# Moving the scaling of the normalised keys one doubling level earlier in VectorE's order

## The chip, the cores and the metric

The kernel runs on one core of a Trainium2 chip. The metric is the device time of one execution in microseconds (us), smaller is better. Two kernels are compared by the medians of runs that alternate on one chip.

## What is computed

The whole program is two networks, one after the other, each of depth 2, on 512 tokens of width 1024. The change lies in one part of the first network: the RWKV layer, a recurrence with a 64x64 state for each of 16 heads, run forward (d = 0) and backward (d = 1) over 256 context tokens and then 512 tokens. In short:

```python
kk = to_heads((k * k_k).astype(jnp.float32))
kk = kk * lax.rsqrt(jnp.sum(kk * kk, axis=-1, keepdims=True) + 1e-12)
...
def step(s, inp):                       # for each token, each head
    r_t, w_t, k_t, v_t, a_t, b_t = inp  # a_t = -kk, b_t = kk * a
    sa = jnp.einsum('bhvk,bhk->bhv', s, a_t)
    s = s * w_t[:, :, None, :] + sa[..., None] * b_t[:, :, None, :] + v_t[..., None] * k_t[:, :, None, :]
    return s, jnp.einsum('bhvk,bhk->bhv', s, r_t)
```

The normalised key `kk` is the quantity that matters here: both `a_t` and `b_t` of the recurrence are made of it. Mixture-of-experts layers stand before and after this part, and the second network (four kinds of attention and a feed-forward layer) follows.

## The kernel before

**Tiling.** The RWKV part works on pairs of heads, 128 channels at a time: `for p in range(KT)` with KT = 8, and in it `for d in range(2)`, the two directions. I call one (p, d) a half; there are 16. Tokens are cut into 12 chunks of 64 (NCH), handled in three groups b = 0, 1, 2 of four chunks (GC). While the chunks of direction d are being inverted and combined, the small vectors of the other direction, a = 1 - d, are prepared, so the two kinds of work alternate on every engine.

**The levels.** The triangular system of each chunk is inverted by doubling, in levels l = 1 to 5. For each level and each group, TensorE makes products (`level_products`, through the helper at line 1378) into a PSUM bank, VectorE masks the bank into the tile T (`level`, line 2768), TensorE makes two more products from T (`double_products`), and ScalarE copies them back (`level_copy`, line 2221). I write T(l,b) and XX(l,b) for them. The T banks are `"T": (2, 3, 2)`: T(l,2) uses the same PSUM bank as T(l,0). So TensorE may not start T(l,2) until VectorE has read T(l,0), and XX(l,0) needs T(l,0) too; the wait stands inside the loop over the middle levels:

```python
if b == 2:
    pe.wait_ge(lv_dve, i * 3 + ts)
```

**The order of the work.** Each engine runs its own list in order. `RK_DVE`, `RK_ACT`, `RK_PE` and `RK_POOL` write the order of the named steps out by hand; `rk_done(engine, p, step)` turns a step into a count of that engine's semaphore, which others wait for. The T and XX steps count on semaphores of their own.

**The keys.** At p, with d = 1, ScalarE squares the keys (line 2136), TensorE sums the squares by head, ScalarE takes logs (line 2156), and later, after its copies of level 1, does three things in this order: `key_factors` (line 2151, step `ka`), `key_roots` (line 2166, step `kr`: exp(-0.5 x) of the log, the reciprocal root) and `variance_roots` (line 2175, step `rs`). VectorE's `normed_keys` (line 2792, step `kkn`) waits for `kr` and multiplies the tile `kn` of 128x768 by the keys. Two consumers wait for `kkn`:

- GpSimd's `raw_keys`: it first waits for `ka` and multiplies `kd` by the keys (line 3246), then waits for `kkn` and multiplies `bd` by `kn` (line 3248). Behind it stand `keys_summed` (line 3254), `decayed_keys` (lines 3262 and 3263, which wait for ScalarE's step `exps`) and `decayed_queries` (line 3268).
- VectorE's own `decayed_sums` (line 2798), at level 3, which also waits for `exps`.

Both feed TensorE's `scores`, which come after level 5.

**Around it on VectorE.** At level 1 of a half stand the T steps, three steps of the sequential chain between chunks (`chain`, line 2776, named z) and `scan` (line 2783). With d = 1, level 2 is T(2,0), T(2,1), T(2,2), `normed_keys`, `normed` (line 2823, step `yn`, which belongs to the output of the previous pair), and then level 3 begins.

Of the kernel before, what the change touches and what calls it, by code (L numbers as in the profile page):

```python
# [100 lines left out]
for _d in range(2):  # L101
    _a = 1 - _d
    _z = [("z", _a, _j) for _j in range(1, 12)]
    _zs = lambda n: [_z.pop(0) for _ in range(min(n, len(_z)))]
    RK_PE += [("vt", 0), ("vt", 1)] if _d == 0 else []
    RK_PE += [("x0", _d, 0), ("pre", _a, 0), ("pre", _a, 1), ("x0", _d, 1), ("x0", _d, 2)] + _zs(1)
    RK_PE += [("mv", _d, 0)] + _zs(1) + [("mv", _d, 1)] + _zs(1) + [("mv", _d, 2)] + _zs(1)
    RK_PE += [("kn", 0)] * _d + _zs(_d) + [("kn", 1), ("var",)] * _d
    for _l in range(1, 6):
        _n = _l in (1, 5)  # L110
        RK_PE += [("T", _d, _l, 0), ("T", _d, _l, 1)] + _zs(_n) + [("T", _d, _l, 2), ("XX", _d, _l, 0)] + _zs(_n)
        RK_PE += [("XX", _d, _l, 1)] + _zs(_l == 5) + [("XX", _d, _l, 2)] + _zs(_n)
    RK_PE += [("gate",), ("bonus",)] * _d
    assert not _z
    RK_PE += [("sb", _a, 0), ("sk", _a, 0), ("wu", _d, 0), ("ba", _a, 0), ("kt", _a, 0), ("sb", _a, 1), ("sk", _a, 1)]
    RK_PE += [("wu", _d, 1), ("wu", _d, 2)] + ([] if _d else [("mean",)]) + [("ba", _a, 1), ("kt", _a, 1)]
    RK_PE += [("ar", _d, 0), ("kv", _d, 0), ("sb", _a, 2), ("sk", _a, 2), ("bc", _d, 0), ("ar", _d, 1), ("kv", _d, 1)]
    RK_PE += [("ba", _a, 2), ("kt", _a, 2), ("bc", _d, 1), ("y", _d, 1), ("kv", _d, 2), ("ar", _d, 2), ("bc", _d, 2), ("y", _d, 2)]

    RK_DVE += [("pp",)] if _d else []  # L120
    _z = [("z", _a, _j) for _j in range(1, 11)] + [("yf", _a)]
    RK_DVE += [("et", _d)] + [("x0", _d, _b) for _b in range(3)] + _zs(EARLY[_d])
    for _l in range(1, 6):
        _more = {1: [[("scan", _a)], []], 2: [[("kkn",), ("yn",)] * _d, []], 3: [[("ara", _a)], []], 4: [[], [("res1",), ("lnx",)] if _d else [("ksr",)]], 5: [[], []]}[_l]
        RK_DVE += _zs(_l in (1, 5)) + _zs(_l in (1, 5)) + _more[0] + _zs(_l in (1, 5)) + _more[1] + _zs(_l == 5)
    assert not _z
    RK_DVE += [("res",), ("bonus",)] * _d + [("mt", _a, 0)]
    RK_DVE += [("mt", _a, 1)] + ([] if _d else [("cen",)]) + [("ar", _d, 0), ("mt", _a, 2), ("bc", _d, 0)]
    RK_DVE += [("ar", _d, 1), ("bc", _d, 1), ("y", _d, 1), ("ar", _d, 2), ("bc", _d, 2), ("y", _d, 2), ("zi", _d)]

    RK_ACT += [] if _d else [("vt", 0), ("vt", 1)]
    RK_ACT += [("pw", _a), ("pa", _a), ("pwc", _a), ("pac", _a)] + [("kq",)] * _d
    RK_ACT += [("mv", _d, _b) for _b in range(3)] + [("kn", 0), ("kn", 1), ("var",)] * _d
    RK_ACT += [("ka", _a)] + [("kr",), ("rs",)] * _d + [("exps", _a)] + [("aff",)] * _d
    RK_ACT += [("nt", _a, 0), ("wu", _d, 0), ("ba", _a, 0), ("kt", _a, 0), ("nt", _a, 1), ("wu", _d, 1), ("wu", _d, 2)]
    RK_ACT += [("ba", _a, 1), ("kt", _a, 1)] + ([] if _d else [("sq",)]) + [("nt", _a, 2), ("ba", _a, 2), ("kt", _a, 2)]

    RK_POOL += [("kdk", _a), ("bdk", _a), ("ksm", _a), ("bds", _a), ("kds", _a), ("arr", _a), ("qm", _a, 1), ("qm", _a, 2)]
    LV_DVE += [("T", _d, _l, _b) for _l in range(1, 6) for _b in range(3)]
    LV_ACT += [("XX", _d, _l, _b) for _l in range(1, 6) for _b in range(3)]  # L140
    LV_POOL += [("nl", _d, _b) for _b in range(3)] + [("ni", _d, _b) for _b in range(3)]
# [76 lines left out]
for _u in range(len(ATTENTION)):  # L218
    _more = _u + 1 < len(ATTENTION)
# [180 lines left out]
def build(nc, slabs_d, vecs_d, tabs1_d, tabs2_d, aux_d, lora_d, x_d, ctx_d, out_d, kv_d):  # L400
# [5 lines left out]
    with stack:  # L406
# [48 lines left out]
        def cut(whole, at, *shape):  # L455

            n = math.prod(shape)
            v = whole[:, at:at + n]
            if len(shape) == 2:
                v = v.rearrange("p (a b) -> p a b", a=shape[0])  # L460
            if len(shape) == 3:
                v = v.rearrange("p (a b c) -> p a b c", a=shape[0], b=shape[1])
            return v
# [117 lines left out]
        lnx, o = cut(work, o, 2), o + 2  # L581
# [21 lines left out]
        ksr, o = cut(work, o, NX), o + NX  # L603
# [173 lines left out]
        def rk_done(engine, p, *name):  # L777

            order = {"pe": RK_PE, "dve": RK_DVE, "act": RK_ACT, "pool": RK_POOL}[engine]
            return {"pe": rk_pe, "dve": rk_dve, "act": rk_act, "pool": rk_pool}[engine], rk_count(order, p, name)  # L780
# [1649 lines left out]
        def _(v):  # L2430
# [100 lines left out]
            for f in range(KT):  # L2531
                for part in range(2):
# [10 lines left out]
                    d = v.drain()  # L2543
# [194 lines left out]
            def column(n):  # L2738
                return pp[:, n:n + 1]
# [5 lines left out]
            def parameters(p):  # L2745

                v.tensor_copy(lnxn, pp[:, 7:9])
                v.drain()
                v.tensor_copy(pp[:, 0:9], rwp[:, bass.ds(p + 1, 1), :].rearrange("p a b -> p (a b)"))
                v.drain()  # L2750
                v.tensor_scalar(column(9), column(5), -1.0, 1.0, ALU.mult, ALU.add).then_inc(rk_dve, rk.next("pp"))

            def totals(p, d):

                v.wait_ge(*rk_done("act", p - 1 if d == 0 else p, "exps", d))
                v.tensor_copy(ETd[d], ETa[d]).then_inc(rk_dve, rk.one("et", d))

            def first_levels(p, d):

                for b in range(3):  # L2760
                    v.wait_ge(*rk_done("pe", p, "x0", d, b))
                    v.tensor_tensor(X[:, GC * b:GC * b + GC, :], rk_bank("x0", d, b)[:, 0:256].rearrange(CHUNKED, c=GC),
                                    bc(eye2.unsqueeze(1), 128, GC, CH), ALU.add).then_inc(rk_dve, rk.one("x0", d, b))
# [25 lines left out]
            def normed_keys(p):  # L2789

                v.wait_ge(*rk_done("act", p, "kr"))
                v.scalar_tensor_tensor(kn, ktile, column(4), kn, ALU.mult, ALU.mult).then_inc(rk_dve, rk.next("kkn"))
# [92 lines left out]
            for p in range(KT):  # L2885
                for d in range(2):
                    a = 1 - d
                    if d == 1:
                        parameters(p)
                    totals(p, d)  # L2890
                    first_levels(p, d)
                    for j in range(1, EARLY[d] + 1):
                        chain(p, a, j)
                    steps = iter(range(EARLY[d] + 1, NCH))
                    for l in range(1, 6):
                        level(p, d, l, 0)
                        level(p, d, l, 1)
                        if l in (1, 5):
                            chain(p, a, next(steps))
                        level(p, d, l, 2)  # L2900
                        if l in (1, 5):
                            chain(p, a, next(steps))
                        if l == 1:
                            scan(p, a)
                        elif l == 2 and d == 1:
                            normed_keys(p)
                            normed(p)
                        elif l == 3:
                            decayed_sums(p, a)
                        if l in (1, 5):  # L2910
                            chain(p, a, next(steps))
                        if l == 5 and d == 0:
                            chain(p, a, next(steps))
                        if l == 4:
                            if d == 1:
                                with_bonus(p)
                                v.tensor_copy(lnx, lnxn).then_inc(rk_dve, rk.one("lnx"))
                            else:
                                weighted_keys(p)
                    if d == 1:  # L2920
                        gated(p)
                        bonuses(p)
                    masked_scores(p, a, 0)
                    masked_scores(p, a, 1)
                    if d == 0:
                        centred(p)
                    transitions(p, d, 0)
                    masked_scores(p, a, 2)
                    additions(p, d, 0)
                    for b in (1, 2):  # L2930
                        transitions(p, d, b)
                        additions(p, d, b)
                    first_state(p, d)
                assert rk.rest() == 0
# [605 lines left out]
```

## Time and profile before

| | |
|---|---|
| median of 3 runs | 4296.15 us |
| lowest, highest run | 4291.41, 4308.15 us |
| the profiled execution's own time | 4308.15 us |
| its span, first to last instruction | 4306.3 us |
| TensorE busy, share of the span | 3907.4 us, 91% |
| VectorE, ScalarE, GpSimd busy | 38%, 20%, 17% |
| the RWKV halves | from about 1240 to 2028 us of the span |

Busy time is the time in which an engine executes something; an engine that is idle because another is late is not busy. What an engine waited for is given as the releaser: the engine and line whose end let it go on. "Issue" is TensorE waiting for nothing that the profile names. The profile prints rows with line numbers of the kernel; TensorE's products all carry the line of a helper (1378 for pairs of heads, 907 for plain products), so their place is read from the time and from the engines around them.

### The profile page before, as it was taken

The page shows a single profiled execution, that of the slowest core. Times are in us where ns is not written, and L with a number is a line of the kernel's source. Part 1 is how long each engine was busy: PE and PEld are TensorE (multiplying, and loading weights), DVE is VectorE, ACT ScalarE, POOL GpSimd, SP SyncE. Part 2 cuts the span into 40 slices and gives each one's busy share as a digit, 9 for nine tenths or more (in the row PEclk, how much of TensorE's full clock was granted, in tenths as well). Part 3 has the DMA queues.
Part 4 walks back from the last instruction along what each step waited for, and adds up shares of the span by engine and source line. Part 5 has one row for each costly group of instructions (what it writes and reads, how often), then busy time and mean ns, then how long its engine had stood idle before and what let it go on. Part 6 is the DMA issues. An engine that isn't in the chain of part 4 may idle for free.

```text
span 4306.3 us, 93568 instructions
## 1 busy us (share of the span) xinstructions
PE 3907.4 (91%) x39960; PEld 2506.7 (58%) x39960; DVE 1636.1 (38%) x3343; ACT 850.4 (20%) x1847; POOL 750.8 (17%) x601
## 2 busy tenths in 40 slices
PE   5979999989978888888899998999999989999998
PEld 4534444445557777777344443456688854658887
DVE  2412112144445554444222222453444425516353
ACT  2200000020045555444100001214000011420000
POOL 4100000000033433333000000000334300004343
PEclk8989999999989999999899999999999999999999
DMA  8287887862200000000379995110222211002221
GB/s 336 98 305 298 334 332 298 334 253 92 81 7 12 12 17 12 12 12 12 137 330 429 429 429 244 40 59 1 79 79 81 94 69 47 32 20 84 93 79 39
DMA packets 54202, 619.10 MB, mean 144 GB/s; under 512 B 5648, under 2 KB 8976, under 8 KB 18320
## 3 DMA queue, kind: packets, MB, share of 16 engines
q1 hardware_dynamic: 49664, 599.41, 35.3%
q10 hardware_dynamic: 2448, 9.05, 0.6%
q0 software_dynamic: 1792, 6.29, 0.5%
q8 instruction: 234, 3.83, 0.4%
q14 instruction: 64, 0.52, 0.0%
HBM read 602.40 MB, written 12.32 MB: 143 GB/s over the span
## 4 chain that ended last, share of the span: by engine, by line
PE 44%; issue 43%; DVE 4%; DMA 3%; POOLq 3%; POOL 2%; ACT 1%; DVEq 1%; PEld 0%; SPq 0%; ACTq 0%; PEldq 0%
PE bank L907 30%; PE bank L1378 13%; DMA ring<-slabs 2%; POOL work L3316 1%; POOLq L3319 1%; POOLq L3317 1%; DMA kv<-work 1%; POOLq L3206 1%; POOL work L3320 1%; PE bank L1429 1%; DVE work L2768 1%; DVE work L2448 0%; DVE hc L2508 0%; DVE hc L2509 0%; PEld bank L907 0%
## 5 line engine op out<-in xcount | busy, mean ns | idle before, releaser
L907 PE MATMUL bank<-ring,work 128*32 128x256 f32 (+3 forms) x7002 | 764.0, 438 | 69.4 <-DMA ring<-slabs 57.3
L907 PE MATMUL bank<-work 128*128 128x256 f32 (+8 forms) x3590 | 782.0, 428 | 26.4 <-DVE work L3132 16.7
L907 PEld LDWEIGHTS bank<-work 128*128 128x128 f32 (+3 forms) x3590 | 499.0, 184 | 298.4 <-issue 213.5
L907 PEld LDWEIGHTS bank<-ring,work 128*32 128x32 f32 (+2 forms) x7002 | 316.5, 123 | 491.8 <-issue 394.6
L907 PE MATMUL bank<-work,ring 128*128 128x256 f32 (+1 forms) x1616 | 482.6, 457 | 13.4 <-DVE work L3151 5.1
L907 PE MATMUL bank<-hx,ring 128*128 128x512 f32 (+1 forms) x1344 | 482.8, 515 | 6.6 <-DVE hx L2463 4.5
L907 PEld LDWEIGHTS bank<-work,ring 128*128 128x128 f32 x1616 | 307.1, 191 | 183.9 <-issue 135.0
L907 PEld LDWEIGHTS bank<-hx,ring 128*128 128x128 f32 x1344 | 255.9, 192 | 221.3 <-issue 200.4
L1378 PE MATMUL bank<-work 64*64 64x64 f32 x11520 | 322.8, 225 | 63.4 <-issue 48.5
L1378 PEld LDWEIGHTS bank<-work 64*64 64x64 f32 x11520 | 288.8, 138 | 91.1 <-issue 88.7
L3209 POOL TENSOR_TENSOR work<-work 128x512 f32<-128x512 f32 (+1 forms) x30 | 34.4, 1155 | 1470.2 <-ACT work L1980 1470.2
L2439 DVE TENSOR_TENSOR work<-work,bank 128x256 f32<-128x256 f32 x240 | 91.8, 416 | 396.0 <-ACT work L2417 391.7
L2417 ACT ACTIVATE work<-bank 128x256 f32<-128x256 f32 x48 | 18.4, 383 | 725.3 <-PE bank L907 725.3
L2221 ACT ACTIVATE work<-bank 128x512 f32<-128x512 f32 (+1 forms) x240 | 127.8, 553 | 166.2 <-PE bank L1378 163.3
L3315 POOL TENSOR_TENSOR work<-ring 128x512 f32<-128x512 f32 (+1 forms) x48 | 78.7, 1640 | 459.8 <-PE bank L907 429.9
L2768 DVE TENSOR_TENSOR work<-bank,tabs_sb 128x256 f32<-128x256 f32 x240 | 100.9, 424 | 121.0 <-PE bank L1378 118.0
L1378 PE MATMUL bank<-ring,work 64*64 64x64 f32 (+1 forms) x3168 | 113.7, 250 | 34.2 <-issue 19.0
L2656 DVE TENSOR_TENSOR work<-work,bank 128x256 f32<-128x256 f32 x16 | 6.8, 422 | 323.9 <-PE bank L907 323.9
L3132 DVE SCALAR_TENSOR_TENSOR work<-work 128x256 f32<-128x256 f32 x176 | 123.6, 717 | 16.3 <-issue 6.8
L907 PE MATMUL bank<-resc,work 128*128 128x256 f32 x512 | 121.3, 380 | 4.3 <-POOL work L3315 3.9
L1378 PEld LDWEIGHTS bank<-ring,work 64*64 64x64 f32 x3168 | 97.1, 137 | 47.9 <-issue 46.8
L907 PE MATMUL bank<-hx,work 128*128 128x256 f32 x512 | 121.1, 379 | 0.4 <-POOL work L3316 0.4
(320 smaller groups left out, 4781.6 us busy)
## 6 DMA issues: line engine op xcount, KB each, us to landing
ring<-slabs SPq DMA_DIRECT2D x228, 2048.0 KB, 9.7
work<-slabs SPq DMA_DIRECT2D x48, 2048.0 KB, 18.3
work<-kv SPq DMA_DIRECT2D x18, 384.0 KB, 3.1
kv<-work SPq DMA_DIRECT2D x2, 3072.0 KB, 15.7
kv<-work ACTq DMA_DIRECT2D x6, 512.0 KB, 17.7
work<-tabs ACTq DMA_DIRECT2D x1, 2176.0 KB, 8.7
resx<-xT SPq DMA_DIRECT2D x1, 2048.0 KB, 11.1
outT<-hx ACTq DMA_DIRECT2D x8, 256.0 KB, 2.1
```

The source lines that it names most:

```text
L907: return pe.matmul(out, lhsT, rhs, start=(k == 0), stop=(k == n - 1))
L1378: m = pe.matmul(out[other if across else r], lhsT[r], rhs[r], start=first, stop=last)
L1429: pe.matmul(outw[:, 0:n], wa2[two[d], 0:128], HW[two[d], at:at + n], start=True, stop=True)
L2221: act.activation(dst, bank, ACT.Copy).then_inc(lv_act, 1)
L2439: v.tensor_tensor(out, a, b, op)
L2768: v.tensor_tensor(T[d][:, GC * b:GC * b + GC, :], rk_bank("T", d, l, b)[:, 0:256].rearrange(CHUNKED, c=GC), bc(levels[:, 1 - d, l, :].unsq ...
L3132: return v.scalar_tensor_tensor(dst, x, 1.0, y, ALU.mult, ALU.subtract)
L3206: pool.drain()
L3315: pool.tensor_tensor(s3, a["a11"], a["a21"], ALU.subtract).then_inc(ff_pool, 1)
L3316: pool.tensor_tensor(s1, a["a21"], a["a22"], ALU.add).then_inc(ff_pool, 1)
L3317: pool.drain()
L3319: pool.drain()
```

## The change

The call of `normed_keys(p)` moves, on VectorE, from behind T(2,2) of level 2 to the end of level 1, behind the third chain step, ahead of T(2,0). The hand-written order `RK_DVE` moves its step `kkn` in the same way, so that all counts of the semaphore agree. The instruction itself, its operands and its wait for `kr` are the same, and no other engine's list is touched. It concerns the halves with d = 1: eight calls.

```diff
@@ RK_DVE, the order of VectorE's steps
-        _more = {1: [[("scan", _a)], []], 2: [[("kkn",), ("yn",)] * _d, []], 3: [[("ara", _a)], []], ...
+        _more = {1: [[("scan", _a)], [("kkn",)] * _d], 2: [[("yn",)] * _d, []], 3: [[("ara", _a)], []], ...
@@ VectorE, in the loop over the levels
                         if l == 1:
                             scan(p, a)
                         elif l == 2 and d == 1:
-                            normed_keys(p)
                             normed(p)
                         elif l == 3:
                             decayed_sums(p, a)
@@
                             chain(p, a, next(steps))
                         if l == 5 and d == 0:
                             chain(p, a, next(steps))
-                        if l == 4:
+                        if l == 1 and d == 1:
+                            normed_keys(p)
+                        elif l == 4:
                             if d == 1:
                                 with_bonus(p)
```

## Rows read from the trace of the kernel before

**Rows 1.** Busy time and granted clock by stretch: all RWKV halves.
```profile
core 0: us, PE busy (x) PEld busy (x) DVE busy (x) ACT busy (x) POOL busy (x), PEclk, DMA share, GB/s
1240.00:2028.00 788.00, 655.37 (x21942) 570.01 (x21942) 381.85 (x844) 401.76 (x751) 301.52 (x309) 0.98 0.05 13
```

**Rows 2.** Timeline of VectorE, second half of p = 1: start, duration, line.
```profile
1394.62 0.28 DVE L2776 SCALAR_TENSOR_TENSOR work<-bank,work,hc 128x64 f32<-128x64 f32 x1 [1.17 <-PE bank L1378]
1395.14 0.89 DVE L2768 TENSOR_TENSOR work<-bank,tabs_sb 128x256 f32<-128x256 f32 x2 [0.23 <-PE bank L1378]
1396.43 0.42 DVE L2768 TENSOR_TENSOR work<-bank,tabs_sb 128x256 f32<-128x256 f32 x1 [0.40 <-PE bank L1378]
1396.77 1.90 DVE L2792 SCALAR_TENSOR_TENSOR work<-work 128x768 f32<-128x768 f32 x1
1398.59 0.68 DVE L2823 TENSOR_TENSOR work<-work 128x512 f32<-128x512 f32 x1
1399.64 0.89 DVE L2768 TENSOR_TENSOR work<-bank,tabs_sb 128x256 f32<-128x256 f32 x2 [0.37 <-PE bank L1378]
```

**Rows 3.** Timeline of ScalarE, same stretch.
```profile
1394.92 1.03 ACT L2151 ACTIVATE work<-work 128x768 f32<-128x768 f32 x1
1395.84 0.84 ACT L2166 ACTIVATE work<-work 128x768 f32<-128x768 f32 x1
```

**Rows 4.** Timeline of GpSimd, same half.
```profile
1396.03 1.82 POOL L3246 TENSOR_TENSOR work<-work 128x768 f32<-128x768 f32 x1 [13.58 <-ACT work L2151]
1398.75 2.21 POOL L3248 TENSOR_TENSOR work<-work 128x768 f32<-128x768 f32 x1 [0.90 <-DVE work L2792]
...
1405.96 1.73 POOL L3268 TENSOR_TENSOR ring<-work 128x512 f32<-128x512 f32 x1
```

**Rows 5.** Timeline of TensorE, same half: level 2, and the first scores.
```profile
1394.42 2.29 PE L1378 MATMUL bank<-work 64*64 64x64 f32 x67
1396.92 0.96 PE L1378 MATMUL bank<-work 64*64 64x64 f32 x45 [0.21 <-issue]
...
1412.66 1.56 PE L1378 MATMUL bank<-ring,work 64*64 64x64 f32 x48
```

**Rows 6.** Timelines of VectorE and ScalarE: p = 0, 4 and 7, level 2.
```profile
1297.39 0.89 DVE L2768 TENSOR_TENSOR work<-bank,tabs_sb 128x256 f32<-128x256 f32 x2
1298.16 0.83 ACT L2166 ACTIVATE work<-work 128x768 f32<-128x768 f32 x1
...
1693.08 0.41 DVE L2768 TENSOR_TENSOR work<-bank,tabs_sb 128x256 f32<-128x256 f32 x1
1695.64 0.42 DVE L2768 TENSOR_TENSOR work<-bank,tabs_sb 128x256 f32<-128x256 f32 x1 [0.36 <-PE bank L1378]
...
2003.99 0.89 DVE L2768 TENSOR_TENSOR work<-bank,tabs_sb 128x256 f32<-128x256 f32 x2 [0.39 <-PE bank L1378]
2005.62 1.01 DVE L2792 SCALAR_TENSOR_TENSOR work<-work 128x768 f32<-128x768 f32 x1
2003.50 0.83 ACT L2166 ACTIVATE work<-work 128x768 f32<-128x768 f32 x1
```

**Rows 7.** TensorE at p = 0, level 2, and the instruction queue beside it.
```profile
1300.11 1.64 PE L1378 MATMUL bank<-work 64*64 64x64 f32 x65 [1.00 <-issue]
...
q8 instruction: 1, 0.02, 1.9%
```

**Rows 8.** Stretches of p = 5 with TensorE's granted clock, and T(3,0), T(4,0) there.
```profile
1798.00:1801.30 3.30, 1.88 (x51) 1.67 (x53) 1.16 (x3) 2.04 (x5) 2.52 (x2) 1.00 0.00 0
1801.30:1804.70 3.40, 3.40 (x116) 3.33 (x113) 1.30 (x2) 2.13 (x4) 2.67 (x2) 0.50 0.00 0
...
1800.26 0.89 DVE L2768 TENSOR_TENSOR work<-bank,tabs_sb 128x256 f32<-128x256 f32 x2 [1.96 <-PE bank L1378]
1805.07 0.89 DVE L2768 TENSOR_TENSOR work<-bank,tabs_sb 128x256 f32<-128x256 f32 x2 [2.13 <-PE bank L1378]
```

**Rows 9.** Timeline of VectorE, p = 1: T(4,0) and T(4,1).
```profile
1403.65 0.89 DVE L2768 TENSOR_TENSOR work<-bank,tabs_sb 128x256 f32<-128x256 f32 x2 [1.10 <-PE bank L1378]
```

**Rows 10.** Who waited for whom in the RWKV halves: total, times, longest.
```profile
PE bank L1378 <- issue: 105.6, 128, 2.4
```

More of the change, by code:

```diff
@@ L123 @@
     for _l in range(1, 6):
-        _more = {1: [[("scan", _a)], []], 2: [[("kkn",), ("yn",)] * _d, []], 3: [[("ara", _a)], []], 4: [[], [("res1",), ("lnx",)] if _d else [("ksr",)]], 5: [[], []]}[_l]
+        _more = {1: [[("scan", _a)], [("kkn",)] * _d], 2: [[("yn",)] * _d, []], 3: [[("ara", _a)], []], 4: [[], [("res1",), ("lnx",)] if _d else [("ksr",)]], 5: [[], []]}[_l]
         RK_DVE += _zs(_l in (1, 5)) + _zs(_l in (1, 5)) + _more[0] + _zs(_l in (1, 5)) + _more[1] + _zs(_l == 5)
```

## The prediction, made before the changed kernel was run

> **What bounds the kernel now.** I read the busy shares of the RWKV stretch first, then the timelines of the engines over one half with d = 1, then who waited for whom. In the stretch of 788 us TensorE is busy for 655 us, VectorE and ScalarE for about half, GpSimd for 38% [rows 1]. TensorE is the engine whose list sets the end, and most of what it loses it loses to "issue" [rows 10]. But busy VectorE time is not free: TensorE may only go on inside a level when VectorE has emptied T. So the question is where in VectorE's list the instruction of line 2792 is late for somebody, not how long it takes.
>
> At p = 1 VectorE ends chain step z8 at 1394.90, starts T(2,0) at 1395.14, T(2,1) follows, T(2,2) starts at 1396.43, `kkn` (line 2792) at 1396.77 and takes 1.90 us, `yn` ends at 1399.27, and T(3,0) starts at 1399.64, after an idle 0.37 us that TensorE ended [rows 2]. So where `kkn` stands today, it and `yn` fill a hole in which VectorE would wait for TensorE: it costs the path nothing. Its input `kr` on ScalarE ends at 1396.68 [rows 3], 0.09 us before `kkn` starts. The new place is the one before T(2,0), at 1394.90: 1.78 us before its input exists.
>
> **The change part by part.**
>
> *The consumers of kkn.* GpSimd's line 3246 waits for `ka` alone and ends at 1397.85; line 3248 starts 0.08 us after `kkn` [rows 4]. What earlier start can they get? None at p = 1: `kkn` already starts 0.09 us after its input. At p = 4 and p = 7, `kkn` starts behind T(2,2), 1.3 us and more after `kr` (2005.62 against 2004.33) [rows 6], so there it could be up to 1.3 us earlier. But line 3268, the last thing that `scores` needs from GpSimd, ends at 1407.69, and the scores start at 1412.66, when level 5 is through [rows 4, 5]. There are 5 us of slack, so an earlier `kkn` is worth 0. The other consumer, at level 3, waits for `exps` as well, which comes behind level 2. I credit nothing.
>
> *The hole that it leaves.* 0, since T(3,0) was waiting for TensorE [rows 2].
>
> *The new place, p = 1.* VectorE comes to `kkn` at 1394.90 and waits until 1396.68 + 0.09 = 1396.77. So it starts when it started before. Behind it on VectorE now stand T(2,0), T(2,1) and T(2,2), and for T(2,0) TensorE waits twice (the shared bank of T(2,2), and XX(2,0)).
>
> How long does `kkn` take there? Durations are 1.90 us at p = 1 and 1.01 us at p = 7 [rows 2, 6]. At p = 1 GpSimd's line 3246 runs beside it until 1397.85 and `kkn` ends at 1398.67, 0.82 us later [rows 2, 4]. At p = 7 it started 1.3 us after `kr`, when line 3246 was nearly through. Since the new place ties the start to `kr` and line 3246 to `ka`, one ScalarE instruction ahead of it, every pair gets the relation of p = 1. I take 1.90 us for all eight; the bound below is 1.01.
>
> The Trainium skill (SBUF — State Buffer, Who interferes with whom) says that a VectorE instruction with two SBUF inputs and a GpSimd instruction that reads SBUF exclude each other for the whole instruction. By that rule `kkn` cannot end before the GpSimd instruction has ended plus its own work, which is what the 0.82 us at p = 1 look like; without the rule it would be 1.01 us for all.
>
> So T(2,0) starts, by the overlap of 0.08 us that is usual between two VectorE rows, at `kr`'s end + 0.09 + 1.90 - 0.08, that is `kr` + 1.91. From T(2,0) to T(2,2) it is 1.29 us (1395.14 to 1396.43), which is the eviction, the release and TensorE's eight pairs of products [rows 2]. T(2,2) therefore starts at `kr` + 3.20. At p = 1: 1396.68 + 3.20 = 1399.88, against 1396.43: 3.45 us late.
>
> The same for all pairs, from the end of `kr` and the start of T(2,2): p = 0 (1298.99, 1298.68) 3.51; p = 1 3.45; p = 2 3.35; p = 3 2.86; p = 4 (1694.55, 1695.64) 2.11; p = 5 2.84; p = 6 1.65; p = 7 (2004.33, 2005.28) 2.25 [rows 2, 3, 6]. At p = 4 TensorE's own stall had already pushed T(2,2) 2.56 us behind T(2,0) [rows 6], so part of the wait is hidden there. Sum 22.0 us. Everything behind T(2,2) hangs on it in a chain (XX, copy, next T), and `exps`, GpSimd and the scores move along by the same amount, so I see no slack in the half that gives it back. One stall of 0.4 us in level 2 of p = 1, after a fetch of instructions that is by then over, drops out: the row at 1396.92 [rows 5]. That leaves **21.6 us**.
>
> *The clock.* TensorE now stands still for about 3.4 us in level 2. In the trace of before, such breaks bring its clock down: at p = 5 TensorE was busy for 1.88 of 3.30 us, and in the next 3.40 us the granted clock was 0.50, 1.2 GHz in place of 2.4 GHz [rows 8]. What one such stretch costs: T(3,0) to T(4,0) took 4.81 us there and 4.01 us at full clock at p = 1 [rows 2, 8, 9]: 0.80 us. The bounds are none more, and two more per half (16 x 0.80 = 12.8 us). I take six: at p = 6 and p = 7 there is a stretch at half clock already, and elsewhere the break will mostly be long enough. 6 x 0.80 = **4.8 us**.
>
> Sum: 21.6 + 4.8 = **+26.4 us**. The profiled execution took 4308.15 us and would take 4334.6. It is itself 12 us above the median of 4296.15, so I set the sum on the median: **4322.5 us**, a ratio of 1.006.
>
> **The rivals.** 0.5% is 21.5 us, and about the least that a measurement of this kernel can tell from no change; I use it as the border.
>
> *A. TensorE's fetches of instructions hide part of the wait.* For this speaks that TensorE in this stretch idles for "issue" 128 times, 105.6 us in all [rows 10]. An example is the 1.00 us before 1300.11, level 2 of p = 0, with one packet of the instruction queue just before it [rows 7]. Stalls of this kind, of 1.0 to 1.5 us, stand behind T(2,2) at p = 0, 5, 6 and 7, about 5 us together. If the fetch went on while TensorE waits, these would be gone: 22.0 - 0.4 - 5 = +16.6 us, and with fewer breaks at half clock about +19, so 4315. Against it: the fetch of p = 0 starts after TensorE has passed the wait for T(2,0), so it is tied to the place in the code, and the place doesn't move.
>
> The Trainium skill (Runtime: NRT & Kernel Launch, Instruction fetch mechanics) says that the sequencer fetches the next block while it executes the present one and that this is mostly hidden. The trace disagrees on "hidden", with its 105.6 us of issue.
>
> *B. kkn takes 1.01 us in its new place.* Then each delay is 0.89 us less: 22.0 - 7.1 = +14.9 us, and with shorter breaks and two or three stretches at half clock +17, so 4313. For this speak the rows of 1.01 us, against it the relation to line 3246 above.
>
> *C. The change does next to nothing.* This would be if the 5 us of slack before the scores belonged not to GpSimd alone but to TensorE, that is if something else than the chain of levels set the start of the scores. I see nothing in the rows that does. It would give 0 to +5 us, 4299.
>
> *D. Faster.* One mechanism: GpSimd's lines 3248, 3262, 3263 and 3268 set the start of the scores in the later pairs, where `kkn` gets up to 1.3 us earlier. It would decide if line 3268 ended at the start of the scores and not 5 us ahead, and if `kr` were there before z8 ends. Price: at most 3 pairs x 1 us, -3 us, 4293, and only with the loss at T(2,0) away. The row of `kr` speaks against it at every pair.
>
> **How the numbers follow.** Chances: the forecast (wait in full, some half clock; its own range +20 to +34 us, 4316 to 4330) 0.65; A 0.15; B 0.09; C 0.08; D 0.03. For the range, the lower end must take in B and A with some of the spread between executions (the three runs lie 17 us apart), the upper end two more half-clock stretches per half (21.6 + 12.8 = +34.4): 4307 to 4331, which leaves out C, D and a little of the ends. Slower by over 0.5% needs more than +21.5 us: most of the forecast's share (0.85 of it), and a third of A's and a tenth of B's: about 0.62. The rest of these and C are within 0.5%: 0.35. Faster: 0.03.
>
> **What the new profile would show.** In the halves with d = 1: `kkn` directly behind z8 with 1 to 2 us of idle VectorE time before it, released by ScalarE's line 2166, in eight places; its duration near 1.90 us in all eight; T(2,0) directly behind it, with no idle time; from the end of `kr` to the start of T(2,2) 3.20 us; TensorE idle 3 us or more ahead of T(2,2), named as released by VectorE or as issue; and more stretches at clock 0.50 right behind. GpSimd's line 3248 starts no earlier relative to `kr`. The halves with d = 0 and everything outside 1240 to 2028 us keep their length. I am wrong if `kr` comes earlier on ScalarE than today (nothing in ScalarE's list changes), if `kkn` takes 1.0 us there, if the issue stalls behind T(2,2) vanish, or if the halves grow by less than T(2,2) is late.

## The result, and the profile after

| kernel | median, us | range, us | runs |
|---|---|---|---|
| before | 4296.41 | 4289.33 to 4308.15 | 8 |
| after | 4317.77 | 4302.49 to 4331.86 | 8 |

The ratio is 1.0051, with a 95% interval of 1.0035 to 1.0068: the changed kernel is 21.4 us slower. The first experiment, with other runs of both kernels, gives 1.0048, 1.0027 to 1.0068. The forecast was 4322.5 us. The profiled execution of after took 4321.99 us; its span is 4320.2 us. In the changed kernel GpSimd's lines 3246, 3248 and 3268 have the numbers 3247, 3249 and 3269; VectorE's and ScalarE's lines named here keep theirs.

VectorE's timeline of after, second half of p = 1, answers to [rows 2]. Columns: start, duration, line, in brackets the idle time before and who ended it.

```profile
1396.73 0.28 DVE L2776 SCALAR_TENSOR_TENSOR work<-bank,work,hc 128x64 f32<-128x64 f32 x1 [2.08 <-PE bank L1378]
1398.61 1.93 DVE L2792 SCALAR_TENSOR_TENSOR work<-work 128x768 f32<-128x768 f32 x1 [1.60 <-ACT work L2166]
1400.46 0.74 DVE L2768 TENSOR_TENSOR work<-bank,tabs_sb 128x256 f32<-128x256 f32 x2
1401.74 0.42 DVE L2768 TENSOR_TENSOR work<-bank,tabs_sb 128x256 f32<-128x256 f32 x1 [0.54 <-PE bank L1378]
1402.08 0.91 DVE L2823 TENSOR_TENSOR work<-work 128x512 f32<-128x512 f32 x1
1404.99 0.42 DVE L2768 TENSOR_TENSOR work<-bank,tabs_sb 128x256 f32<-128x256 f32 x1 [2.01 <-PE bank L1378]
```

The third chain step ends, VectorE stands idle for 1.60 us until ScalarE's line 2166 (`kr`) is there, `kkn` takes 1.93 us, and T(2,0) follows with no idle time. Before, `kkn` and `yn` filled VectorE's wait for TensorE; now VectorE waits there 2.01 us and the time is empty.

GpSimd's timeline of the same half, for [rows 4]:

```profile
1397.92 1.80 POOL L3247 TENSOR_TENSOR work<-work 128x768 f32<-128x768 f32 x1 [14.96 <-ACT work L2151]
1400.62 1.82 POOL L3249 TENSOR_TENSOR work<-work 128x768 f32<-128x768 f32 x1 [0.90 <-DVE work L2792]
```

ScalarE's, for [rows 3]:

```profile
1397.75 0.83 ACT L2166 ACTIVATE work<-work 128x768 f32<-128x768 f32 x1
```

`kkn` starts 0.03 us after `kr` ends (1398.58) and ends 0.82 us after GpSimd's line 3247 does (1399.72), as at p = 1 before. GpSimd's line 3249 starts 2.04 us behind the end of `kr`, against 2.07 before (1398.75 against 1396.68) [rows 3, 4]: the consumer gets nothing.

All instructions of line 2792 in after (count, then minimum, median and maximum duration in ns), and the idle time before them:

```profile
L2792 DVE SCALAR_TENSOR_TENSOR work<-work x9: 1932/1935/1941, 1214.4 to 2022.5; 128x768 f32<-128x768 f32 x9
its engine sat idle before it (us, times) until:
  ACT work L2166: 16.1, 9
```

Nine, since one belongs to the prologue: 1.93 us in every one.

TensorE, after. The first row is from p = 1, the second from p = 0; the idle time in brackets is the break in level 2.

```profile
1401.02 6.16 PE L1378 MATMUL bank<-work 64*64 64x64 f32 x224 [2.98 <-DVE work L2768]
...
1299.80 5.41 PE L1378 MATMUL bank<-work 64*64 64x64 f32 x155 [3.63 <-DVE work L2768]
```

Busy time by stretch, after, p = 0: the break, and what follows it. Columns as in [rows 1]; the tenth is TensorE's granted clock.

```profile
1296.20:1299.60 3.40, 0.00 (x0) 0.00 (x0) 2.22 (x3) 1.67 (x3) 2.02 (x2) 1.00 0.02 5
1299.60:1303.00 3.40, 3.20 (x97) 3.16 (x101) 1.74 (x4) 0.91 (x2) 2.17 (x2) 0.50 0.02 5
```

The same at p = 1, where the break ends at 1401.02:

```profile
1398.60:1402.00 3.40, 0.98 (x51) 1.01 (x55) 2.85 (x4) 0.49 (x1) 2.50 (x2) 1.00 0.00 0
1402.00:1405.40 3.40, 3.40 (x104) 3.33 (x97) 1.39 (x3) 2.42 (x4) 1.46 (x2) 0.50 0.03 7
```

At p = 0 TensorE stands still for the whole of the first stretch and runs the second at half clock (0.50, 1.2 GHz). From T(2,0) to T(2,2) it is 1.71 us there (1299.24 to 1300.95). At p = 1 that piece is still at full clock and takes 1.28 us (1400.46 to 1401.74), as it did before [rows 2]; half clock follows 0.98 us after the break.

From p = 4 on the idle time is in two pieces, since a stall for instructions stands just ahead of the break. TensorE at p = 5:

```profile
1815.61 0.62 PE L1378 MATMUL bank<-work 64*64 64x64 f32 x13 [1.07 <-issue]
1818.55 2.72 PE L1378 MATMUL bank<-work 64*64 64x64 f32 x78 [2.33 <-DVE work L2768]
```

**Where the time went.** The RWKV stretch, measured in each trace from the first instruction of VectorE's line 2762 to the last T(5,0), before:

```profile
1236.70:2018.04 781.34, 650.43 (x21808) 566.07 (x21810) 379.08 (x839) 400.90 (x749) 304.54 (x314) 0.98 0.04 13
```

after:

```profile
1235.02:2038.17 803.15, 659.54 (x21818) 576.14 (x21822) 386.07 (x840) 401.94 (x749) 302.98 (x314) 0.96 0.04 12
```

Who TensorE waited for there, in us, times, longest; before:

```profile
PE bank L1378 <- issue: 105.0, 127, 2.4
PE bank L1378 <- DVE work L2768: 6.6, 14, 1.6
```

after:

```profile
PE bank L1378 <- issue: 100.7, 117, 2.8
PE bank L1378 <- DVE work L2768: 25.1, 15, 3.6
```

Each kernel was profiled a second time (the first and the fifth experiment). The means of the two profiles:

| in the RWKV stretch, us | before | after | difference |
|---|---|---|---|
| length | 782.0 | 804.1 | +22.1 |
| TensorE waits for line 2768 (T) | 6.2 | 25.9 | +19.7 |
| TensorE waits for issue | 105.2 | 99.2 | -6.0 |
| TensorE busy, same products | 652.1 | 661.9 | +9.8 |
| of it at half clock (counted in the trace's record of the clock) | 39.3 | 76.8 | +37.5 |

The three differences make +23.5 of the +22.1 us. The halves with d = 1 together went from 384.4 and 380.5 us to 405.0 and 405.6, those with d = 0 from 396.9 and 402.1 to 398.2 and 399.5. Outside the stretch nothing changed in one direction. The two first profiles differ by only 13.9 us in span because there after was 1.7 us shorter ahead of the stretch and 6.2 us behind it; the stretch holds what the medians show.

### The profile page after: what moved, and what is told of

Same layout as the page of the kernel before. It is cut to its first block, busy times and chain, and to the rows that moved or that the text cites. A ratio compares the mean times of both kernels' runs of the same rounds, so it can differ in the third digit from the quotient of the medians.

```text
span 4320.2 us, 93568 instructions
## 1 busy us (share of the span) xinstructions
PE 3907.6 (90%) x39960; PEld 2505.7 (58%) x39960; DVE 1642.4 (38%) x3343; ACT 851.3 (20%) x1847; POOL 749.6 (17%) x601
## 4 chain that ended last, share of the span: by engine, by line
PE 44%; issue 43%; DVE 4%; DMA 3%; POOLq 3%; POOL 2%; ACT 1%; DVEq 1%; PEld 0%; SPq 0%; ACTq 0%; PEldq 0%
PE bank L907 30%; PE bank L1378 13%; DMA ring<-slabs 2%; POOL work L3317 1%; POOLq L3320 1%; POOLq L3318 1%; DMA kv<-work 1%; POOLq L3207 1%; POOL work L3321 1%; PE bank L1429 1%; DVE work L2768 0%; DVE work L2792 0%; DVE work L2448 0%; DVE hc L2508 0%; DVE hc L2509 0%
## 5 line engine op out<-in xcount | busy, mean ns | idle before, releaser
L1378 PE MATMUL bank<-work 64*64 64x64 f32 x11520 | 332.6, 232 | 80.3 <-issue 47.1
L1378 PEld LDWEIGHTS bank<-work 64*64 64x64 f32 x11520 | 300.6, 143 | 107.4 <-issue 104.8
L3210 POOL TENSOR_TENSOR work<-work 128x512 f32<-128x512 f32 (+1 forms) x30 | 34.4, 1156 | 1465.8 <-ACT work L1980 1465.8
L1378 PE MATMUL bank<-ring,work 64*64 64x64 f32 (+1 forms) x3168 | 111.3, 248 | 31.5 <-issue 17.0
L3133 DVE SCALAR_TENSOR_TENSOR work<-work 128x256 f32<-128x256 f32 x176 | 123.6, 717 | 16.3 <-issue 6.8
```

The source lines that it names most:

```text
L1378: m = pe.matmul(out[other if across else r], lhsT[r], rhs[r], start=first, stop=last)
L3133: return v.scalar_tensor_tensor(dst, x, 1.0, y, ALU.mult, ALU.subtract)
```

## The experiments

The ratio is always to the kernel before, timed in turn with it on the same chip; its median there was 4299.32 us beside experiments 1 to 4, 4296.60 beside 5 to 8, and 4301.99 beside 9 and 10. The ratio is not exactly that of the two medians. The stretch is the one above; means of two profiles for before and after, one profile for the others.

| experiment | median, us | ratio, 95% interval | stretch | waits for T | half clock |
|---|---|---|---|---|---|
| before | 4296.41 | | 782.0 | 6.2 | 39.3 |
| after | 4317.77 | 1.0051, 1.0035 to 1.0068 | 804.1 | 25.9 | 76.8 |
| 1 after again | 4318.23 | 1.0048, 1.0027 to 1.0068 | (in after) | | |
| 2 wait only | 4308.90 | 1.0012, 0.9995 to 1.0029 | 787.8 | 11.8 | 47.8 |
| 3 kr early | 4303.03 | 1.0003, 0.9989 to 1.0018 | 782.5 | 9.1 | 34.1 |
| 4 GpSimd late | 4318.54 | 1.0037, 1.0018 to 1.0055 | 792.3 | 22.1 | 44.4 |
| 5 before again | 4298.66 | 0.9995, 0.9976 to 1.0013 | (in before) | | |
| 6 after, unrolled | 4333.72 | 1.0088, 1.0060 to 1.0115 | 816.4 | 31.5 | 88.7 |
| 7 6 with filler | 4317.08 | 1.0050, 1.0032 to 1.0069 | 803.8 | 16.3 | 37.5 |
| 8 before, unrolled | 4298.18 | 1.0004, 0.9986 to 1.0021 | 776.5 | 4.5 | 41 |
| 9 behind the scan | 4306.77 | 1.0008, 0.9994 to 1.0023 | 777.3 | 7.5 | 37.5 |
| 10 copy late | 4298.41 | 0.9998, 0.9977 to 1.0020 | 777.8 | 2.1 | 27.3 |

### 1 and 5. Both kernels again

No edit. They show how far two profiles of one kernel lie apart in the sums above.

> The changed kernel itself once more, for a second profile of it. Theory (the wait): T(2,0) stands on VectorE behind an instruction whose input comes late; T(2,2) starts 3.6 us after kr ends in all eight halves with d = 1, kkn takes 1.93 us, and the halves with d = 1 are together 20 us longer than before, while the rest of the program differs only by what two executions of one kernel differ. Rival (the loss is spread, by the clock): the 20 us would be found in other places than in the first profile. Time expected: 4318 us, ratio 1.005.

> The kernel before itself, for a second profile of it. It says how far two executions of one kernel differ in the RWKV halves: from the first row of line 2762 to the last T(5,0) it was 781.3 us in the first profile, against 803.2 and 806.4 us in the two profiles of the changed kernel. Theory (the difference is the change's): within 4 us of 781. Rival (half of it is chance): near 790. Ratio 1.000.

After: +18.9 us, stretch 805.1 us (the second expectation, written later, gives 806.4). From the end of `kr` to T(2,2) it is 3.60, 3.17, 3.60, 3.61, 3.61, 3.54, 3.17 and 3.61 us, so the 3.6 us expected in all eight halves come in six, and in the first profile in seven (p = 1 has 3.16). The 20 us are again in the halves with d = 1. Before against itself: 0.9995. The same kernel has a stretch of 781.3 or 782.6 us, 803.2 or 805.1 us. Two profiles each show the spread only in part: experiments 8, 9 and 10, whose times are those of before, have stretches of 776.5 to 777.8 us. A difference of under 5 us in one profile is therefore not read as a gain or a loss.

### 2. The wait without the work

```diff
 # the kernel before, VectorE, level 1, behind the third chain step
+                        if l == 1 and d == 1:
+                            v.wait_ge(*rk_done("act", p, "kr"))
```

> Half of the move: VectorE waits for kr at the new place, ahead of T(2,0), but kkn itself is executed at its old place behind T(2,2). Theory (wait and work both count): T(2,0) starts 0.1 us after kr's end and T(2,2) 1.4 us after it; from the trace of before that is late by 1.7, 1.6, 1.5, 1.0, 0.3, 1.0, 0 and 0.4 us, 7.6 us in all, and kkn takes 1.0 us since line 3246 on GpSimd is through: 4304 us, ratio 1.0018. Rival (the wait for kr is all of it, and kkn's work hides behind TensorE): ratio 1.005 as in the full change. Rival (it is all kkn's work): no change.

VectorE, p = 0:

```profile
1298.12 0.76 DVE L2768 TENSOR_TENSOR work<-bank,tabs_sb 128x256 f32<-128x256 f32 x2 [1.79 <-ACT work L2166]
1299.41 0.42 DVE L2768 TENSOR_TENSOR work<-bank,tabs_sb 128x256 f32<-128x256 f32 x1 [0.53 <-PE bank L1378]
1299.76 1.01 DVE L2792 SCALAR_TENSOR_TENSOR work<-work 128x768 f32<-128x768 f32 x1
```

VectorE waits as long as in after, T(2,0) starts when `kr` ends, and T(2,2) comes 1.32 us behind it (1.76 at p = 2). The stretch grows by 5.8 us, against 7.6 expected. The ratio makes it some 5 us, with an interval that does not tell it from none; the medians lie 9.6 us apart. `kkn` behind T(2,2) takes 1.01 us in every half, since GpSimd's instruction is by then mostly through. The wait alone is thus about a quarter of the loss, as far as one profile tells.

### 3. The work without the wait

```diff
 # the changed kernel, ScalarE: kr right behind the variance logs, ahead of the level-1 copies and of ka
-    RK_ACT += [("mv", _d, _b) for _b in range(3)] + [("kn", 0), ("kn", 1), ("var",)] * _d
-    RK_ACT += [("ka", _a)] + [("kr",), ("rs",)] * _d + [("exps", _a)] + [("aff",)] * _d
+    RK_ACT += [("mv", _d, _b) for _b in range(3)] + [("kn", 0), ("kn", 1), ("var",), ("kr",)] * _d
+    RK_ACT += [("ka", _a)] + [("rs",)] * _d + [("exps", _a)] + [("aff",)] * _d
                         variance_logs(p)
+                        key_roots(p)
...
                         if l == 1 and d == 1:
-                            key_roots(p)
                             variance_roots(p)
```

> The changed kernel with its input made early: key_roots stands on ScalarE directly behind the logs, ahead of the copies of level 1, where ScalarE waits for TensorE. Theory (wait and work both count): VectorE no longer waits at kkn; kkn starts right behind z8 and takes 1.0 us because it is done before line 3246 on GpSimd starts. T(2,0) is late by about 0.8 us a half and some of it is hidden behind stalls of TensorE: +5 us, 4301 us, ratio 1.0012. Rival (kkn's work is the cost, 1.9 us wherever it stands ahead of T(2,0)): +12 us, 1.003. Rival (something else in the new order than T(2,0) costs, such as GpSimd's earlier line 3248): still 1.005.

VectorE, p = 1:

```profile
1393.78 0.28 DVE L2776 SCALAR_TENSOR_TENSOR work<-bank,work,hc 128x64 f32<-128x64 f32 x1 [1.16 <-PE bank L1378]
1393.97 1.01 DVE L2792 SCALAR_TENSOR_TENSOR work<-work 128x768 f32<-128x768 f32 x1
1394.90 0.75 DVE L2768 TENSOR_TENSOR work<-bank,tabs_sb 128x256 f32<-128x256 f32 x2
```

With its input there, `kkn` starts as soon as the chain step is done, takes 1.01 us, and T(2,0) starts 0.84 us behind the chain step in place of 0.24. The stretch is 782.5 us and the time that of before (5 us more were expected, which the interval still allows). The place in VectorE's list alone is not what costs; it is the place together with an input that is late and a neighbour that blocks.

### 4. GpSimd's instruction behind kkn

```diff
 # the changed kernel, GpSimd
                 pool.wait_ge(*rk_done("act", p, "ka", d))
-                pool.tensor_tensor(kd, kd, ktile, ALU.mult).then_inc(rk_pool, rk.next("kdk", d))
                 pool.wait_ge(*rk_done("dve", p if d == 0 else p - 1, "kkn"))
+                pool.tensor_tensor(kd, kd, ktile, ALU.mult).then_inc(rk_pool, rk.next("kdk", d))
```

> The changed kernel with GpSimd's line 3246 behind the wait for kkn, so that it can't run beside kkn. Theory (kkn's 1.93 us are 1.01 us of work and 0.92 us of waiting for GpSimd's instruction): kkn takes 1.01 us in all eight halves, T(2,2) starts 2.7 us after kr's end in place of 3.6, 7.4 us less than the changed kernel in all and somewhat less half clock; GpSimd starts 2 us later and has 5 us of slack: about +13 us, 4309 us, ratio 1.003. Rival (GpSimd's chain has no slack): ratio 1.005 or more, with TensorE's scores waiting for line 3268.

All instructions of line 2792:

```profile
L2792 DVE SCALAR_TENSOR_TENSOR work<-work x9: 1018/1019/1020, 1213.6 to 2012.7; 128x768 f32<-128x768 f32 x9
```

VectorE at p = 0:

```profile
1295.81 1.02 DVE L2792 SCALAR_TENSOR_TENSOR work<-work 128x768 f32<-128x768 f32 x1 [1.79 <-ACT work L2166]
```

TensorE, p = 0:

```profile
1297.30 1.61 PE L1378 MATMUL bank<-work 64*64 64x64 f32 x80 [2.71 <-DVE work L2768]
```

Busy time by stretch, the break and what follows it:

```profile
1294.50:1297.30 2.80, 0.10 (x4) 0.03 (x1) 1.50 (x3) 1.79 (x3) 0.33 (x1) 1.00 0.03 6
1297.30:1300.70 3.40, 3.05 (x137) 2.84 (x139) 1.53 (x4) 1.82 (x4) 3.40 (x2) 1.00 0.02 5
```

TensorE at p = 5, and its clock there:

```profile
1801.63 0.62 PE L1378 MATMUL bank<-work 64*64 64x64 f32 x13 [0.80 <-issue]
1803.93 2.26 PE L1378 MATMUL bank<-work 64*64 64x64 f32 x80 [1.68 <-DVE work L2768]
...
1801.20:1804.60 3.40, 1.29 (x44) 1.18 (x48) 1.69 (x3) 1.72 (x3) 1.01 (x1) 1.00 0.00 0
1804.60:1808.00 3.40, 2.96 (x97) 2.55 (x86) 1.31 (x2) 1.19 (x2) 3.40 (x3) 0.51 0.02 5
```

`kkn` still waits for `kr`, but takes 1.02 us in place of 1.93: the 0.9 us in each half belong to GpSimd's instruction beside it. The stretch is 792.3 us, 11.8 us less than in after, of which the waits for T give only 3.8 us in the sums, and 8.7 us are TensorE's busy time (653.2 against 661.9 us): behind a break of 2.71 us the granted clock at p = 0 stayed 1.00, and behind after's 3.63 us it was 0.50. It stayed full in the halves p = 0 to 3; in p = 4, 5 and 6, where a stall for instructions of 0.72 to 1.72 us stands ahead, half clock comes 0.6 to 1.0 us behind the end of breaks of only 0.79 to 1.81 us, and in p = 7 between a stall of 1.36 us and the break. The expectation of +13 us for the stretch was 2.7 us high. GpSimd's later work did not become late: its last instruction for the scores ended at 1308.79, the scores began at 1313.76. The times do not show this gain: the ratio of 1.0037 makes it some 16 us over before, against 10.3 in the stretch, the interval overlaps that of after, and the median is 4318.54 us where after, beside it, had 4318.23. That the loss is about halved rests on the stretch of one profile.

### 6. Level 2 written out: the fetches moved

```diff
 # the changed kernel, TensorE, middle levels
+                first = 2 + (d == 1)
+                if d == 1:
+                    level_t(p, d, 2, 0)
+                    level_t(p, d, 2, 1)
+                    level_t(p, d, 2, 2)
+                    for b in range(3):
+                        level_x(p, d, 2, b)
...
-                with pe.Fori(0, 3) as i:
+                with pe.Fori(0, 5 - first) as i:
```

> The changed kernel with TensorE's level 2 of the halves with d = 1 written out ahead of the loop (the loop then runs over levels 3 and 4 alone). The waits are the same; the code is longer by one level per half with d = 1, and the places where TensorE fetches instructions move. It is the control for the next run. Theory: T(2,2) still starts 3.6 us after kr's end, half clock in the RWKV halves stays near 70 to 85 us, ratio 1.005 plus up to 0.002 for eight or so more fetches of about 1 us.

The same products run in the same order, but TensorE's code lies elsewhere, and so do the places at which it runs dry. The changed kernel is now slower than expected: ratio 1.0088 against at most 1.007, stretch 816.4 us, half clock 88.7 us against 70 to 85. What of this is the move of `kkn`, experiment 8 shows.

### 7. The same, with filler products in the break

```diff
 # experiment 6, TensorE
                     level_t(p, d, 2, 1)
+                    pe.wait_ge(*rk_done("dve", p, "z", 0, 8))
+                    for _ in range(4):
+                        mm(P[6][:, 256:512], headones, tab("level")[:, 0:256], 0, 1)
                     level_t(p, d, 2, 2)
```

The four products write a part of a bank that nobody reads; their result goes nowhere. They wait for the third chain step.

> As the run before it, with four products of 128x128 by 256 columns, whose result nobody reads, put between TensorE's T(2,1) and its wait for T(2,0): about 2 us of work inside a wait of 3.8 us. The wait is as long as before; only TensorE's idleness is gone. Theory (a third to a half of the loss is TensorE at 1.2 GHz after the idle stretch): T(2,2) starts 3.2 us after kr in place of 3.6, half clock in the RWKV halves falls to 35 to 45 us, and the kernel is 6 to 9 us faster than the unrolled one. Rival (the clock costs nothing, the wait is all): the same time as the unrolled one.

TensorE, p = 0 (line 2778 is T's line 2768 in this kernel):

```profile
1284.07 1.99 PE L907 MATMUL bank<-tabs_sb 128*128 128x256 f32 x8
1287.91 1.29 PE L1378 MATMUL bank<-work 64*64 64x64 f32 x59 [1.85 <-DVE work L2778]
```

The break is 1.99 us of filler (eight records for the four products) and 1.85 us of idle time in place of one break. VectorE's list, and so its lateness, is that of experiment 6, and the time falls by 16.6 us in the medians and by 12.6 us in the stretch; the time at half clock falls from 88.7 to 37.5 us, that of before. From the end of `kr` to T(2,2) it is 3.17 us in seven halves of eight, where after had 3.60. The expectation was 6 to 9 us. The filler also moves the code behind it, and experiment 8 shows how much a layout can do; but the time for issue went up by 3.0 us (101.1 to 104.1), so that isn't where the gain came from. TensorE's busy time, with about 16 us of filler in it, fell from 665.8 to 663.3 us. So I put 12 us and more of the cost in experiment 6 down to the clock, 0.25 us of stretch for each us at half clock (12.6 by 51.2).

### 8. The kernel before with level 2 written out

The edit of experiment 6 on the kernel before.

> The kernel before with the same unrolling of level 2. With the unrolled changed kernel it gives the cost of the move a second time, in code whose fetches stand elsewhere. Theory: the difference between the two is 18 to 25 us, as between the originals; the unrolling alone costs 0 to 8 us. Rival (the cost of the move depends on where the fetches fall): a difference well under 15 us or over 28 us.

1.0004: writing level 2 out costs nothing by itself. The move of `kkn`, put on top, costs 35.5 us in the medians and 39.9 us in the stretch (776.5 to 816.4), where it costs 21.4 and 22.1 in the first layout. In the parts: waits for T +27.0 us (4.5 to 31.5), busy +17.5 us (648.3 to 665.8), issue -3.3 us (104.4 to 101.1). The rival of this expectation was right. By the busy time a us at half clock is dearer here, 0.37 us (17.5 by 47.7). What such a move costs depends on the layout of TensorE's code, and with it on where TensorE runs dry of instructions by itself.

### 9. kkn behind the scan, with kr early

The kernel before, with experiment 3's edit on ScalarE, and on VectorE:

```diff
                             scan(p, a)
+                            if d == 1:
+                                normed_keys(p)
                         elif l == 2 and d == 1:
-                            normed_keys(p)
                             normed(p)
```

> An earlier place than the change's, with the input early as in the third run: key_roots directly behind the logs on ScalarE, and kkn on VectorE directly behind scan, ahead of chain step z8, where VectorE waits for TensorE in most halves. Theory (a place costs what of wait and work lies beyond the hole it fills): kkn takes 1.01 us, fills VectorE's wait for z8, T(2,0) isn't late, TensorE's waits for line 2768 are about 7 us in the RWKV halves as before, and the ratio is 1.000. Rival (anything of 1 us ahead of T(2,0) costs, input early or not): ratio 1.001 to 1.002.

VectorE, p = 1:

```profile
1392.05 1.77 DVE L2783 TENSOR_TENSOR_SCAN work<-tabs_sb,work 128x780 f32<-128x780 f32 x1
1393.74 0.99 DVE L2792 SCALAR_TENSOR_TENSOR work<-work 128x768 f32<-128x768 f32 x1
1394.99 0.28 DVE L2776 SCALAR_TENSOR_TENSOR work<-bank,work,hc 128x64 f32<-128x64 f32 x1 [0.26 <-PE bank L1378]
1395.51 0.89 DVE L2768 TENSOR_TENSOR work<-bank,tabs_sb 128x256 f32<-128x256 f32 x2 [0.23 <-PE bank L1378]
```

Here `kkn` fills VectorE's wait ahead of the third chain step (0.26 us of it is left) and costs nothing that can be measured: 1.0008, with an interval of 0.9994 to 1.0023 that does not shut out the rival by itself; the stretch of 777.3 us, no longer than before's, speaks against it. I take it as no better than the old place either, since no consumer waits for `kkn`.

### 10. The copy of line 2917 later

The kernel before, with the step `lnx` at the end of level 5 in place of level 4. In the trace of before this copy of 128x2 elements takes 1.24 us in level 4; VectorE's timeline, p = 1:

```profile
1406.48 1.24 DVE L2917 COPY work<-work 128x2 f32<-128x2 f32 x1
```

It ends at 1407.72, and GpSimd's line 3268 ends at 1407.69 [rows 4].

```diff
                                 with_bonus(p)
-                                v.tensor_copy(lnx, lnxn).then_inc(rk_dve, rk.one("lnx"))
...
+                        elif l == 5 and d == 1:
+                            v.tensor_copy(lnx, lnxn).then_inc(rk_dve, rk.next("lnx"))
```

> The kernel before with another instruction moved: the 128x2 copy of line 2917, which takes 1.24 us at level 4 beside GpSimd's line 3263, goes to the end of level 5, where GpSimd is idle. Theory (a VectorE instruction that GpSimd holds up and that stands ahead of a T costs the part that sticks out): the copy takes 0.1 to 0.3 us there, T(5,0) comes up to 0.3 us earlier in the halves with d = 1, 2 us in all: ratio 0.9995, not to be told from 1 by the time, so the profile decides. Rival: the copy is in a hole and nothing moves.

```profile
L2920 DVE COPY work<-work x8: 160/161/163, 1312.3 to 2018.5; 128x2 f32<-128x2 f32 x8
```

The copy takes 0.16 us in its new place, and TensorE's waits for T go from 6.2 to 2.1 us. The stretch is some 4 us shorter (782.0 to 777.8), where 2 us were expected; neither the spread of single profiles nor the time tells it from none: 0.9998, 0.9977 to 1.0020. None of the kernels beats before by what can be measured.

## Why the prediction was right, and where it was not

**The four kernels with a later and later T(2,2)** carry the explanation. The second column is the time from the end of `kr` to the start of T(2,2), mean of the eight halves (and of both profiles, for before and after; in the trace that the prediction reads it is 0.45).

| kernel | T(2,2) behind kr | 8 halves, over before | stretch, over before | half clock |
|---|---|---|---|---|
| before | 0.59 | | | 39.3 |
| wait only | 1.38 | 6.3 | 5.8 | 47.8 |
| wait and 1.02 us of work | 2.31 | 13.7 | 10.3 | 44.4 |
| wait and 1.93 us of work (after) | 3.52 | 23.4 | 22.1 | 76.8 |

In the first two steps 0.9 and 0.6 us of each us of lateness reach the end, with a time at half clock near that of before (34.1 and 44.4 us in its two profiles). In the last step 7.3 of the 9.7 us are GpSimd's 0.9 us beside `kkn`; the rest goes with TensorE at half clock, where T(2,0) to T(2,2) takes 1.7 us in place of 1.28. The stretch grows by 11.8, more than T(2,2) comes late.

**Consumers, worth 0: right.** GpSimd's line 3249 follows the end of `kr` as before. Experiment 9, in which `kkn` is really earlier, gains nothing that the time shows either.

**The hole, worth 0: right.** VectorE idles 2.01 us at the old place at p = 1, and T(3,0) waits for TensorE.

**The start of kkn and its 1.93 us: right** in all eight halves, against 1.90 forecast. Experiment 4 shows the cause: rival B's 1.01 us appear once GpSimd's instruction is out of the way, and not otherwise. The Trainium skill has the rule that a VectorE instruction with two SBUF inputs and a GpSimd instruction that reads SBUF shut each other out (SBUF — State Buffer, Who interferes with whom). The trace agrees with it but for 0.2 us: `kkn` ends 0.82 us after GpSimd's instruction, and takes 1.01 us by itself.

**21.6 us of lateness that nothing gives back: the size is off, and this is the first wrong step.** The waits for T grew by 19.7 us, and issue fell by 6.0 us, 5.5 of them in the halves with d = 1. The prediction held the fetches to be tied to their place in the code, so that a wait could not absorb them. One of the prediction's own signs of being wrong came true with this: the stalls behind T(2,2) at p = 0, 5, 6 and 7 are gone in the first profile. At p = 0 the issue stall of 1.00 us [rows 7] is gone: TensorE runs from 1299.80 without a break. The instruction queue of after, between 1296 and 1299.5 us:

```profile
q8 instruction: 1, 0.02, 2.2%
```

The one packet there moves at 1296.3 us, just inside the break and 2.9 us ahead of T(2,0); the prediction had held against rival A that it comes behind T(2,0). So a fetch does go on while TensorE waits, which is rival A's mechanism. Rival A was priced at about 5 us; its four stalls are 1.00, 0.99, 0.86 and 1.33 us in the trace of before, 4.2 us together. At p = 5 to 7 the fetch comes behind T(2,2) and the stall is gone all the same; there TensorE runs at half clock. That it then uses its instructions more slowly than they come is what I think happens, and no run isolates it; in the second profile of after a stall of 1.09 us stands at p = 6 at half clock. The 0.4 us that the prediction takes off for p = 1 are a misreading of its row, which has 0.21 us.

**The clock, 4.8 us: too small, and the second wrong step.** It was forecast as six stretches of 0.80 us; it is +37.5 us at half clock, eleven stretches of 3.4 us, and +9.8 us of busy time. The price per stretch was about right (0.80 by 3.4 is 0.24 us for each us; 9.8 by 37.5 is 0.26; experiments 6 and 7 give 0.25, though 8 and 6 give 0.37 in the busy time). The count was wrong: all sixteen halves with d = 1 in the two profiles of after have half clock from within the break or shortly behind it. In thirteen it starts early enough to reach T(2,2), which comes 3.54 to 3.61 us behind `kr` in place of the 3.20 forecast; in three, p = 1 of after among them, it starts 1.0 to 1.2 us after the break, and T(2,2) comes at 3.16 or 3.17.

**The sum.** Forecast 21.6 + 4.8 = 26.4. Measured 19.7 - 6.0 + 9.8 = 23.5, with the stretch at +22.1 and the medians at +21.4 and +18.9. The two errors, -7.9 us in the lateness and +5.0 us in the clock, have opposite signs and largely cancel. That the total is closer than its parts is luck. (The shares behind the chance of slower by over 0.5% add up to 0.61, not 0.62.) The sign, the place and the mechanism held. The time was forecast as slower by just over 0.5% and is so at the point, with an interval that reaches under it. Experiments 6 and 8 set a limit on the working: with another code layout the same move costs 39.9 us of stretch, over the forecast's upper bound of 34.4.

**What stays open.** After unrolling, the waits for T grow by 27.0 us and not by 19.7. A part of that is where it starts from: in experiment 8 T(2,2) comes 0.05 us behind `kr` on the mean of the halves and not 0.59, so the move makes it 27.5 us late in all and not 23.4; the rest is not explained. The loss of clock is shown (experiment 7 gives it back with VectorE's list unchanged), but the length of the break does not say by itself where it comes: the clock stayed full behind 2.71 us (experiment 4, p = 0) and fell behind 3.63 us (after, p = 0), and also behind 2.98 us (after, p = 1), behind 2.33 us with 1.07 us of issue ahead of it (after, p = 5) and behind 1.68 us with 0.80 us of issue ahead (experiment 4, p = 5). I have these rows and no rule.

## What to carry to other kernels

Before moving an instruction forward, look for the end of its last input: an engine that works its list in order makes everything behind the instruction wait for it, and here neither the wait (+5.8 us of stretch) nor the work (+0.5 us) was dear by itself, but both in a row were (+10.3 us), and with a blocking neighbour more so (+22.1 us). Put side work of VectorE where it waits for TensorE anyway, and look at what GpSimd does in that moment. A break of TensorE can cost more than its length when the granted clock falls behind it, and less when a stall for instructions would have come next; both have to be read from the trace.

## What the hardware showed that I had not expected

An instruction fetch goes on while TensorE stands in a semaphore wait (the packet at 1296.3 us in after), and with the longer waits 6.0 of 105.2 us of issue went away; how much of that is by this mechanism is not shown. The Trainium skill (Runtime: NRT & Kernel Launch, Instruction fetch mechanics) calls the fetch mostly hidden. With 98 to 108 us of issue in stretches of 777 to 816 us these traces do not agree, as far as issue is fetch.

In experiment 4 TensorE's clock stayed full behind a break of 2.71 us (p = 0) and fell behind breaks of 1.68 us (p = 5) and 0.79 us (p = 6), which had a stall for instructions of 0.80 and of 1.72 us ahead of them.

Four products that nobody reads, 1.99 us of TensorE in a break, took 12.6 us off the stretch over eight halves.

A copy of two elements per partition takes 1.24 us in one place and 0.16 us in another. That the longer one waits for GpSimd, as `kkn` does, was not tested by itself.
